# Routing per row tile inside the output projection of a hybrid encoder layer with a hierarchical mixture of experts

## The reference, cut to what matters

```python
merged = (g_sb * (o_sb @ w_sb_branch) + g_dsa * (o_dsa @ w_dsa_branch))
h = x + merged @ w_out
return h + hier_moe(rms_norm(h, norm2_g), w_group, w_router, w_gate, w_up, w_down)

def hier_moe(h, ...):                       # 544 rows
    group_probs = softmax(xt @ w_group)     # 4 groups
    gp, gi = top_k(group_probs, 1)
    elog = (xt @ w_router) of group gi      # 8 experts in it
    ev, ei = top_k(elog, 2)
    ew = softmax(ev) * gp
    # y = sum over the two chosen experts of ew * (silu(x @ w_gate) * (x @ w_up)) @ w_down
```

## Time and profile before

| what | value |
|---|---|
| median of 3 runs | 936.85 us |
| the profiled execution: device time | 936.06 us |
| its span, first to last instruction | 934.3 us |
| PE busy | 827.5 us (89%) |
| DVE, ACT, POOL busy | 306.3, 224.0, 187.9 us |
| DMA moved | 160.13 MB, mean 171 GB/s |
| mean granted TensorE clock | 0.958 |

### The profile page before, as it was taken

The page is one execution under the profiler, slowest core; times in us unless marked ns, Lnnn a source line. Parts: engine busy times, 40 slices in busy tenths (PEclk is TensorE's granted clock), DMA queues, the critical chain, the costliest instruction groups (busy, mean ns, idle before and its releaser), DMA issues.

```text
span 934.3 us, 11345 instructions
## 1 busy us (share of the span) xinstructions
PE 827.5 (89%) x4438; PEld 505.5 (54%) x4438; DVE 306.3 (33%) x788; ACT 224.0 (24%) x461; POOL 187.9 (20%) x257
## 2 busy tenths in 40 slices
PE   5999999999999998999999999953999988777870
PEld 3464344787666755766666854522555545444530
DVE  4213657996544421223222622235000000000005
ACT  3021331112333332343333500120122211111110
POOL 2223420000423212000000020101244332233230
PEclk9999999999999999999999999975999999999995
DMA  8424020422102001202040851195799999999927
GB/s 284 136 91 121 2 91 1 140 102 87 43 0 85 8 1 38 59 3 89 0 91 2 313 231 45 46 387 201 276 395 391 389 394 381 395 388 396 388 77 290
DMA packets 52422, 160.13 MB, mean 171 GB/s; under 512 B 14032, under 2 KB 16304, under 8 KB 43632
## 3 DMA queue, kind: packets, MB, share of 16 engines
q1 hardware_dynamic: 45184, 145.34, 42.0%
q0 software_dynamic: 7184, 14.06, 4.4%
HBM read 151.35 MB, written 15.86 MB: 179 GB/s over the span
## 4 chain that ended last, share of the span: by engine, by line
PE 70%; DMA 11%; SPq 6%; DVE 4%; POOL 3%; ACT 2%; issue 2%; POOLq 0%; DVEq 0%; ACTq 0%
PE quad L747 24%; PE pair L1078 9%; DMA arena<-in_w_up 6%; PE pair L941 5%; PE pair L1273 4%; PE quad L1273 3%; PE quad L815 3%; DMA xnT<-in_w_up 3%; SPq L680 3%; SPq L684 3%; PE quad L1284 2%; PE pair L737 2%; PE quad L1035 2%; POOL arena L1705 1%; PE pair L862 1%
## 5 line engine op out<-in xcount | busy, mean ns | idle before, releaser
L1273 PE MATMUL quad<-arena,ring_w 128*64 128x256 f32 x512 | 65.4, 413 | 16.5 <-DMA arena<-in_w_up 15.8
L747 PE MATMUL quad<-ring_w,xnT 128*128 128x512 f32 (+1 forms) x192 | 79.4, 554 | 0.0
L1750 POOL DMA_INDIRECT y_d<-ring_w,idx_y x64 | 57.7, 901 | 70.5 <-ACT ring_w L1584 58.4
L941 PE MATMUL pair<-xnT,ring_w 128*128 128x272 f32 x256 | 70.3, 410 | 0.9 <-POOLq L1711 0.9
L1078 PE MATMUL pair<-xnT,ring_w 128*128 128x272 f32 x256 | 65.8, 403 | 0.0
L1273 PEld LDWEIGHTS quad<-arena,ring_w 128*64 128x64 f32 x512 | 41.9, 149 | 35.3 <-issue 20.9
L747 PE MATMUL quad<-xnT,ring_w 128*128 128x280 f32 (+1 forms) x256 | 60.6, 396 | 0.0
L1746 POOL DMA_INDIRECT ring_w<-xn_d,idx_x x32 | 30.9, 966 | 137.4 <-PE pair L1266 53.7
L747 PE MATMUL quad<-arena 128*128 128x512 f32 x128 | 55.4, 593 | 1.2 <-DVEq L2012 1.2
L941 PEld LDWEIGHTS pair<-xnT,ring_w 128*128 128x128 f32 x256 | 46.4, 192 | 16.7 <-issue 7.9
L1078 PEld LDWEIGHTS pair<-xnT,ring_w 128*128 128x128 f32 x256 | 46.5, 189 | 15.3 <-issue 6.9
(11 more groups left out here) (254 smaller groups left out, 1174.0 us busy)
## 6 DMA issues: line engine op xcount, KB each, us to landing
arena<-in_w_gate SPq DMA_DIRECT2D x27, 1024.0 KB, 16.9
arena<-in_w_up SPq DMA_DIRECT2D x27, 1024.0 KB, 25.4
arena<-in_w_down SPq DMA_DIRECT2D x44, 512.0 KB, 17.7
ring_w<-in_w_in SPq DMA_DIRECT2D x8, 2048.0 KB, 8.2
ring_w<-in_w_down SPq DMA_DIRECT2D x15, 512.0 KB, 17.9
xnT<-in_w_gate SPq DMA_DIRECT2D x5, 1024.0 KB, 17.7
xnT<-in_w_up SPq DMA_DIRECT2D x5, 1024.0 KB, 26.6
arena<-in_w_out SPq DMA_DIRECT2D x2, 2048.0 KB, 11.0
```

Source lines behind the costliest of these rows:

```text
L747: last = nc.tensor.matmul(o, l, r, start=i == 0, stop=i == len(mms) - 1)
L941: last = nc.tensor.matmul(bank[6 + job % 2][:, 0:hi - lo], chunk8(6 + cb // 4)[:, k, c0:c0 + P], xT[:, k, lo:hi], start=k == 0, stop=k == ...
L1273: last = nc.tensor.matmul(bank[4 * q + 1][64 * f:64 * f + 64, 0:256].rearrange("p (g c) -> p g c", g=2), xgT[:, q, k, :], wv[:, :, k, P * ...
L1750: pool.indirect_dma_start(y_d, bass.IndirectOffsetOnAxis(ap=rows, axis=0), Yb[64 * c:64 * c + 64, q, :], None, bounds_check=4 * NTOK - 1, ...
```

## The change

The order of tiles becomes ORDER = [4, 0, 1, 2, 3]: the sample rows first. Within the output projection PE now does, between the two halves of a tile, the turning of the tile before and the count of places of the one before that, and behind the second half the router product of the tile before and the list entries of the one before that. The router product holds the rows (128 columns) and streams the 36 router columns, so the logits stand as rows in PSUM and need no copy and no turning back. DVE's choices are per tile, 17 instructions, straight from PSUM. `earlier` is kept by one subtraction per tile instead of a scan. The row lists of the 32 first blocks come directly from the place in the expert (a place of 64 or more matches no slot), accumulated over the tiles in bank 7; the last two tiles' entries are made together. Everything on overflow (blocks, slots, weights of the two choices) comes on DVE after the indices, and PE makes the overflow part of the lists after the second expert's gate/up product, DVE its indices after the second hidden product.

Loads: w_out goes to xnT and the ring (earlier: after the 48th gate product); experts 0 to 3 are given space in `arena` that is free when attention is done, with gate/up loaded before the merging ends and down after the last branch product; 4 and 5 after the last output product. The residual rows are loaded as their space comes free, the sample's after 14 of 16 merges, and each tile waits only for its own.

```diff
-    chunk_at = [wslot[s] for s in slots] + [arena[:, 0:4096], arena[:, 4096:8192]]
+    chunk_at = [wslot[s] for s in slots] + [xnT[:, 0:4096], wslot[0]]
...
     # SP
+    sp.wait_ge(pvd_done, NT)
+    for n in range(4):
+        load_gate_up(n, n, gu_in[n])
+    sp.wait_ge(pj_ready, pj_used[9])
+    for n in range(4):
+        for j in range(2):
+            if (n, j) == (1, 1):
+                sp.wait_ge(merged_ready, 16)
+            load_down(n, n, j, dn_in[n])
+    sp.wait_ge(pj_ready, pj_used[13])
+    for n in range(4, MS):
+        load_gate_up(n, n, gu_in[n])
+        for j in range(2):
+            load_down(n, n, j, dn_in[n])
...
     # PE
+    def routed(i):
+        r = TOK[ORDER[i]]
+        pe.wait_ge(tr_free_act, emptied(TR, "act", T_X2 + 2 * i + 1))
+        pj_job([(x2T[:, i % 2, k, 0:r], wr[:, k, :]) for k in range(KT)], lambda b: b[0:r, 0:36])
+    def places(i):
+        pe.wait_ge(marks_ready, i + 1)
+        if i:
+            nc.tensor.matmul(bank[6][:, NE * i:NE * (i + 1)], nones, earlier[:, i, :], start=True, stop=True,
+                             skip_group_check=True)
+        nc.tensor.matmul(bank[6][:, NE * i:NE * (i + 1)], stri, marks[:, i, :], start=i == 0, stop=True,
+                         skip_group_check=True).then_inc(pos_ready, 1)
...
+    output_sample()
+    for i in range(1, NT):
+        output_half(ORDER[i], 0)
+        x2_turned(i - 1)
+        if i >= 2:
+            places(i - 2)
+        output_half(ORDER[i], 1)
+        routed(i - 1)
+        if i >= 2:
+            entries(i - 2)
+    x2_turned(NT - 1)
+    routed(NT - 1)
+    for i in (NT - 2, NT - 1):
+        places(i)
+    for i in (NT - 2, NT - 1):
+        entries(i)
...
     # POOL
+    pool.wait_ge(gd_ready, 32)
+    residual(0)
+    residual(1)
+    pool.wait_ge(merged_ready, 4)
+    pool.dma_start(g2b, ...)
+    pool.wait_ge(merged_ready, 8)
+    residual(2)
+    pool.wait_ge(merged_ready, 14)
+    for g in range(4):
+        pool.dma_start(X[DEC * g:DEC * (g + 1), NT - 1, 256 * g:256 * (g + 1)], ...)
+    residual(3)
...
     # DVE
+    for i in range(NT):
+        output_rows(i, 0)
+        if i >= 2:
+            if i >= 4:
+                dve.wait_ge(idx_part, i - 3)
+            row_ids(i - 2, i % 2)
+            slots(i - 2, i % 2, 1)
+        if i:
+            output_rows(i, 1)
+        nc.vector.sem_inc(h_ready, 1)
+        if i == 0:
+            dve.wait_ge(g2_in, 16)
+        second_norm(i)
+        if i:
+            choices(i - 1)
+    choices(NT - 1)
+    tt(gx[:, 40:40 + NT], v_top[1], v_top[0], ALU.subtract)
+    nc.vector.sem_inc(rvals_ready, 1)
+    dve.wait_ge(idx_part, NT - 2)
+    for j in range(2):
+        row_ids(NT - 2 + j, j)
+    slots(NT - 2, 0, 2)
...
+    dve.wait_ge(idx_part, NT)
+    indices(idx_in, 0, NE)
```

The new per-tile functions on DVE:

```diff
+    def choices(i):
+        r = TOK[ORDER[i]]
+        n = J_RT[i]
+        lg = bank[n % 4][0:r, 0:36]
+        dve.wait_ge(pj_ready, n + 1)
+        top, first, sel, m, e = v_max[0:r, i:i + 1], v_first[0:r], g_eq[0:r], masked[0:r], eq[0:r]
+        red(top, lg[:, 0:NG], ALU.max)
+        stt(sel, lg[:, 0:NG], top, iom[0:r, 0:NG], ALU.is_equal, ALU.mult)
+        red(first, sel, ALU.min)
+        ts(sel, iom[0:r, 0:NG], first, -BIG, ALU.not_equal, ALU.mult)
+        tt(m.rearrange("p (g e) -> p g e", g=NG), lg[:, NG:].rearrange("p (g e) -> p g e", g=NG), ..., ALU.add)
+        ts(gx[0:r, NG * i:NG * (i + 1)], lg[:, 0:NG], top, None, ALU.subtract)
+        nc.vector.sem_inc(pj_free_dve, 1)
+        for c in range(2):
+            top = v_top[c][0:r, i:i + 1]
+            red(top, m, ALU.max)
+            stt(e, m, top, iom[0:r, 0:NE], ALU.is_equal, ALU.mult)
+            red(first, e, ALU.min)
+            ts(oh[0:r, c, i, :], iom[0:r, 0:NE], first, None, ALU.is_equal)
+            if c == 0:
+                stt(m, oh[0:r, 0, i, :], -BIG, m, ALU.mult, ALU.add)
+        tt(marks[0:r, i, :], oh[0:r, 0, i, :], oh[0:r, 1, i, :], ALU.add)
+        tt(earlier[:, i + 1, :], earlier[:, i, :], marks[:, i, :], ALU.subtract)
+        nc.vector.sem_inc(marks_ready, 1)
```

More of the change, by code:

```diff
@@ L41 @@
 TOFF = [P * t for t in range(NT)]
+ORDER = [NT - 1] + list(range(NT - 1))
 NTOK = SEQ + DEC
@@ L1255, in _, with output_half, output_sample @@
-            for n in range(2 * NT):
-                last = nc.tensor.matmul(bank[1][0:CAP, 0:NBLK], at_slot[:, n, :], at_block[:, n, :],
-                                        start=n == 0, stop=n == 2 * NT - 1)
-            last.then_inc(idx_ready, 1)
+            pe.wait_ge(wr_in, 32)
+            def output_half(t, c):
+                c0 = columns(t)[0][2]
+                pj_job([(merged[:, k, c0:c0 + P], chunk8(12 + c)[:, k, :]) for k in range(KT)], lambda b: b[:, :])
+            def output_sample():
+                pj_wait_free(pe, pj[0])
+                b = bank[pj[0] % 4]
+                for k in range(KT):
+                    for g in range(4):
+                        last = nc.tensor.matmul(b[DEC * g:DEC * (g + 1), 0:256], merged[:, k, N_PROMPT:N_ROWS],
+                                                chunk8(12 + g // 2)[:, k, 256 * (g % 2):256 * (g % 2 + 1)],
+                                                start=k == 0, stop=k == KT - 1)
+                last.then_inc(pj_ready, 1)
+                pj[0] += 1
@@ new lines, in places, with entries @@
+            def places(i):
[5 more added lines that the diff above has]
+                                 skip_group_check=True).then_inc(pos_ready, 1)
+            def entries(i):
+                r = TOK[ORDER[i]]
+                pe.wait_ge(slots_ready, i + 1)
+                j = (i + 1) % 2 if i >= 3 else i % 2
+                for c in range(2):
+                    last = nc.tensor.matmul(bank[7][0:CAP, 0:NE], slot_at[0:r, j, c, :], rid_at[0:r, j, c, :],
+                                            start=i == 0 and c == 0, stop=i == NT - 1 and c == 1, skip_group_check=True)
+                last.then_inc(idx_part, 1)
@@ new lines, in _, with over_entries @@
+            nc.tensor.matmul(bank[6][:, NE * NT:NE * (NT + 1)], nones, earlier[:, NT, :], start=True, stop=True,
+                             skip_group_check=True).then_inc(pos_ready, 1)
+            def over_entries():
+                pe.wait_ge(over_slots_ready, 1)
+                for n in range(2 * NT):
+                    last = nc.tensor.matmul(bank[7][0:CAP, NE:NBLK], at_slot[:, n, :], at_block[:, n, :],
+                                            start=n == 0, stop=n == 2 * NT - 1, skip_group_check=True)
+                last.then_inc(over_idx_ready, 1)
```

366 lines of the change are left out of this document (148 added, 218 removed).

## The result

The changed kernel takes 927.4 us (median of 4 runs, 926.82 to 927.73), the kernel before 937.16 beside it (4 runs, 936.07 to 937.52): ratio 0.9897, 95% interval 0.988 to 0.9914.

The account below looks back on a forecast made before the run. The path to the first gate/up product's end, which starts the full expert weight stream, was taken to set the time. Path -10.35 plus list products +1.3 gave -9.05 us from the median 936.85: 927.8, own range 925.5 to 931.

Parts of the forecast that it names:

- The end moves with E: E is the end of the first gate/up product, releasing expert 6's slot; afterwards weights stream at a fixed 8.99 us per expert.
- The path to E: From merged branches (545.93) to the first gate/up product's end: 110.9 us before, ending at 646.5 instead of 656.86 after.
- Router product: Per-tile product of rows with router weights on TensorE: 1.8 us at full clock, 3.5 for the last at the lower clock.
- The wait at the first turning: TensorE waits 1 us for the sample rows' residual and norm before turning the first tile; bounds 0 and 5.8.
- VectorE within a tile: Per-tile choices, 17 instructions in 3.6 us, finish before TensorE asks for them: cover 1.7 us, no stall.
- rival B: TensorE keeps the higher clock through the last router product: turning 1.0 and router 1.8 us less, 925.0 us; chance 0.13.
- Overflow work off the path: VectorE's overflow lists move behind the indices: 9.7 us, done at 645.2, wanted at 646.9, so covered by 1.7.
- Its worth is 0, at worst a few tenths for a gather: Loading expert weights ahead buys nothing by itself, since the stream was already full from the first gate/up product's end.
- The overflow list products, +1.3: TensorE's 20 list products behind the second expert's gate/up delay expert 6's down load, losing 1.3 us once (0 to 2.4).
- Rival A: Sample rows' residual takes 12.6 us to land, so TensorE waits 5.8 us instead of 1: 932.6 us; chance 0.13.
- Rival D: Small VectorE instructions cost 0.42 us instead of 0.21, choices overrun TensorE's cover by 1.9 a tile: 939.7 us; chance 0.09.
- Rival C: First gate/up ends earlier but the stream does not, from a longer last-tile chain or late loads: 936.9 us; chance 0.05.

Follow-up runs that it names:

- experiment 8: Changed kernel with the sync queue's order in the experts' loop made gate/up n + 1, down n: 921.04 us, ratio 0.982 to the kernel before.
- experiment 9: Kernel before with only the sync queue's order for experts 6 to 31 made gate/up n + 1, down n: 932.86 us, ratio 0.9954.
- experiment 1: Changed kernel with the two index instructions put behind all overflow work on VectorE again: 939.11 us, ratio 0.9999 to the kernel before.
- experiment 5: Changed kernel with 27 unread extra products on TensorE in idle stretches between last output product and first gather: 925.58 us, ratio 0.9866 to the kernel before.
- experiment 2: Kernel before, routing still batched, with row lists straight from the places and overflow work moved behind the indices: 934.7 us, ratio 0.9963.
- experiment 10: Changed kernel with TensorE's 20 overflow list products and VectorE's overflow indices moved from expert 1 to expert 25: 928.23 us, beside 928.04 for the changed kernel.
- experiment 7: Changed kernel with the sample rows' residual issued last, after 16 merges instead of 14: 935.98 us, ratio 0.9982 to the kernel before.
- experiment 6: Changed kernel with 17 more small VectorE instructions in the choices of each of the first three tiles: 949.42 us, ratio 1.0129 to the kernel before.
- experiment 4: Changed kernel with no expert loaded ahead, all six slots loading after the output projection's last product: 944.94 us, ratio 1.0086 to the kernel before.
- experiment 3: Changed kernel with two experts loaded before the output projection ends instead of four: 931.67 us, ratio 0.9928 to the kernel before.

## Why the prediction was right, point by point

**The end moves with E: right.** In the ten profiled executions that leave the stream's order alone and load something ahead, before and after included, E lies between 644.47 and 666.60, and E to the last gate/up is 242.1 to 243.7. Only the order of the loads (236.7 to 237.8) or a stream already full at E (255.3) changes it. One row was misread: the gate/up at 890.68 is that of the last expert but one; the last one in before starts at 899.03. So "26 experts, 8.99 each" is 25 experts and 9.35, and "a tail of 44" holds an expert more. The forecast used only the difference, and was not touched: the same product stands at 882.02 after, near the 881 named. Nor was the stream full from E on, as the prediction had it: from 650 to 660 its share is 0.74, and with another order of the loads the same stretch is 6.2 us shorter (experiment 8). It is 5.3 shorter in the kernel before too (experiment 9), so the difference came out even so.

**The path to E: right to 0.1 us, and that is in part luck.** From the last merges to E I had 100.6 and it took 100.6, but up to the last output product it was 1.5 shorter than reckoned (no wait, a cheaper first router product), from there to the indices 0.7 longer, and from the indices to E 0.8 longer.

**Output product, turning at full clock, places: right.** A half takes 7.07 to 6.96 (6.87), the sample 3.66, and the last product ends at 615.7, for 616.6.

**Router product: right where it counted.** At the lower clock 3.65 (3.5), at the higher 1.87 (1.8), from the timeline:

```profile
565.24 0.72 PE L755 MATMUL quad<-small,ring_w 128*32 128x36 f32 x16
...
615.55 1.87 PE L755 MATMUL quad<-small,ring_w 128*128 128x36 f32 x16
```

The first tile has only 32 rows and took 0.72, which I had priced as a full one. No run has the old form of this product in the new order, so what turning it round is worth by itself is not shown.

**The wait at the first turning: 0 instead of 1.** The adds of the sample rows begin at 550.85, when the residual has landed, 0.7 after the product; it took 5.4 to 6.4 us, so the row of 6.4 was the right one to go by. The normalised rows are ready at 556.3, and TensorE comes to them at 557.25: 0.9 to spare.

**VectorE within a tile: right that there is no wait, thinner than I said.** Timeline of VectorE in the choices of the last tile:

```profile
628.80 0.24 DVE L2054 TENSOR_SCALAR small<-small 128x32 f32<-128x32 f32 x1
...
629.30 0.19 DVE L2062 TENSOR_REDUCE small<-gate 128x1 f32<-128x32 f32 x1
```

Those that read a value per row take 0.22 to 0.25, the others 0.16 to 0.19. Seventeen take 4.15 us and not 3.6 (626.57 to 630.73). In the first tile they end at 573.60, and TensorE comes to the places at about 573.7: the cover there is a tenth of a us. In the later tiles it is about 1.2.

**The clock in the tail: right.** Turning 1.98 for 1.9, router product 3.65 for 3.5. For the turning 1.98 is the upper end: behind the same wait of 2.5 us it took 1.19 in experiment 1 and 1.16 to 1.98 over all runs with the same tail. The router product took 3.6 in every one of them. So rival B, that the clock stays up through it, is out, and experiment 5 shows what it would have been worth, 3.9 us to E and not 2.8, since the first gate/up would gain too. That product took 6.08 and not 5.42 as in the earlier trace rows: this is the 0.6 by which E, at 647.15, missed 646.5. The indices were as predicted (634.90 + 0.17 = 635.07 for 635.25).

**Overflow work off the path: right, and without it there is no gain; but it is not the whole cause** (experiments 1 and 2). The prediction summed both changes in one path and did not say what each is worth: together they bring 9.8 at E, this one alone 4.0, the routing per tile alone 0.8. VectorE works on it from 635.08 to 644.8 (predicted 645.2), its next work is wanted at 647.5:

```profile
644.65 0.14 DVE L2237 CAST over_i<-rt 1x1 int32<-1x1 f32 x1
...
647.53 0.29 DVE L2241 TENSOR_TENSOR cst<-cst,quad 128x128 f32<-128x128 f32 x1 [2.74 <-ACT cst L1604]
```

**"Its worth is 0, at worst a few tenths for a gather": wrong.** I saw that the loads end before E, and not that a gather stands between. With two experts ahead the gather takes 6.5 instead of 3.2 us, and the kernel 2 to 3 us more; with none ahead the gather takes 7.8, and the kernel 17 to 18 more, most of it from the stream (12.4 from E on). The Trainium skill, DMA: Bandwidth & Descriptors, section Queues, rings and completion order, which I had weighed for the sample rows, has each engine take turns between queue rows. In the page of the profile the weights are in q1 (145.33 MB) and what GpSimd issues in q0 (14.06 MB), so the gather does not stand behind the weights in their queue, and it still took twice as long. The measurement fits taking turns, and doesn't prove it; what it shows is that a small transfer in another queue was not free.

**The overflow list products, +1.3: not found.** The down load of expert 6 came 1.1 us later after E, as reckoned (9.4 for 8.3), but taking the products away gave nothing back (experiment 10). The 0.8 by which E to the last gate/up exceeds before lies inside the spread of that stretch. What absorbs the 1.1 us stays open. With it left out the sum would have been -10.35, against medians of -9.8 (first set) and -9.0 (last set), so the time forecast, 927.8 for 927.4, owes part of its closeness to it.

**Rival A, a late residual, was priced too low:** the wait of experiment 7 was 5.6 for the 5.8 that it named, but with the clock's share the path grew by 8.9 us and the time by 7 to 8 by the ratios, not 4.8. **Rival D** likewise: its mechanism is real (experiment 6), its 1.9 us a tile left the clock out; in the changed kernel the small instructions start 0.24 apart, far below its 0.39. **Rival C** needs loads that are still running at E; experiment 4 is that case, and there the gain is gone.

## What to carry to other kernels

Find the release that starts the saturated stream and count only the path to it. Two changes on that path can be worth more together than one by one: here 0.8 and 4.0 apart, 9.8 together, so test each with and without the other. On a queue that works in order put no load behind a wait that ends later than its own, and put last what is needed last: here the two together brought 5 to 6 us from E on, more than half of what the whole change did. Price a wait of TensorE with the slow product behind it, and a small gather by whether bulk loads are in flight beside it.

## What the runs showed of the hardware

- After TensorE had stood for 4.2 and 3.3 us in mid-kernel, the granted clock was 0.53 and 0.50 over the next 6 us and a half product took 9.4 and 9.5 instead of 7.0; after 5.6 us it was 0.50, with 17.65 instead of 14.78 for the 48 products behind it. Each wait cost its own length and 2.9 to 3.3 us more, hardly depending on how long it was.
- After a wait of 2.5 us the same eight transposes took between 1.16 and 1.98 us from run to run.
- Products that nobody reads, set into the gaps, kept the granted clock at 0.83 and then 1.00 where it had been 0.50 (experiment 5).
- An indirect gather of 64 rows took 3.2 us when little else moved (share 0.22), and 6.5 and 7.8 us at a share of 1.0 (experiments 3 and 4).
- A VectorE instruction on 128x32 elements takes 0.19 us, and 0.24 to 0.25 with an operand per row.
